# A transformer and state-space block kernel: sums of squares taken in two steps, and unread products in two norm gaps

## What is computed

```python
def rmsnorm(x, g):
    y = x * rsqrt(mean(x * x, axis=-1) + 1e-6)      # mean over the 1024 channels of a token
    return y * g

# first block
...
x = x + rmsnorm(merged @ w_out, norm_mix_post)                 # "post1"
h = rmsnorm(x, norm_mlp_pre)                                   # "n2"
f = square(relu(h @ w_ff_in)) @ w_ff_out
x = x + rmsnorm(f, norm_mlp_post)                              # "post2"
# second block
xn = rmsnorm(x, norm_mix_g_2)                                  # "n3"
...
x = x + merged @ w_out_2
xn2 = rmsnorm(x, norm_ffn_g_2)                                 # "n4"
x = x + (silu(gate) * up) @ w_ffn_out_2
return rmsnorm(x, norm_final_g_2)                              # "n5"
```

## Time and profile before

| | |
|---|---|
| median of three executions | 1516.6 us (1515.08 to 1518.08) |
| the profiled execution, its own time | 1520.02 us |
| its span, first to last instruction | 1518.2 us |
| TensorE (PE) busy | 1435.4 us, 95% |
| VectorE (DVE) busy | 885.6 us, 58% |
| ScalarE (ACT) busy | 626.0 us, 41% |
| mean granted TensorE clock | 0.979 of full |
| chain that ended last | PE 73%, DVE 14%, ACT 9% |

### The profile page before, as it was taken

How to read it: one execution, slowest core, us unless ns; L and a number is a source line. 1 busy time by engine, 2 the same in 40 slices (tenths; PEclk the granted TensorE clock), 3 DMA queues, 4 the chain that set the end, 5 groups by cost and what they waited for, 6 DMA issues and landing times.

```text
span 1518.2 us, 17724 instructions
## 1 busy us (share of the span) xinstructions
PE 1435.4 (95%) x7240; PEld 1155.3 (76%) x7240; DVE 885.6 (58%) x1274; ACT 626.0 (41%) x980; POOL 1.9 (0%) x7
## 2 busy tenths in 40 slices
PE   6999999998999999998999999688899999999997
PEld 5777677777788888887777677576778888888886
DVE  6887644646636354456548786678864443443445
ACT  5452653333313122224326666778743221232232
POOL 0000000000000000000000000000000000000000
PEclk9999999999999999998999999999999999999998
DMA  4222123231333323232121111122232332333232
GB/s 160 84 84 87 55 70 125 85 109 34 111 92 96 105 89 106 86 103 89 58 81 56 56 50 63 38 75 83 71 105 88 97 106 89 97 98 101 94 96 98
DMA packets 36560, 131.62 MB, mean 87 GB/s; under 512 B 4432, under 2 KB 4560, under 8 KB 36224
## 3 DMA queue, kind: packets, MB, share of 16 engines
q1 hardware_dynamic: 36128, 127.16, 26.5%
q0 software_dynamic: 352, 3.34, 0.6%
HBM read 128.39 MB, written 2.10 MB: 86 GB/s over the span
## 4 chain that ended last, share of the span: by engine, by line
PE 73%; DVE 14%; ACT 9%; issue 2%; DMA 1%; SPq 0%; DVEq 0%; ACTq 0%
PE gp L1372 21%; PE gp L1374 21%; PE gp L1373 21%; DVE w_lo L794 2%; PE mp L1548 1%; ACT arena L717 1%; PE mp L1559 1%; PE mp L1517 1%; ACT w_hi L423 1%; DVE arena L1028 1%; PE mp L1398 1%; ACT a_hi L447 1%; ACT arena L572 1%; DVE arena L1035 1%; ACT arena L721 1%
## 5 line engine op out<-in xcount | busy, mean ns | idle before, releaser
L1372 PE MATMUL gp<-a_hi,w_hi 128*128 128x512 f32 x1120 | 444.4, 397 | 14.8 <-DVE arena L1265 13.5
L1373 PE MATMUL gp<-a_lo,w_hi 128*128 128x512 f32 x1120 | 439.7, 393 | 0.0
L1374 PE MATMUL gp<-a_hi,w_lo 128*128 128x512 f32 x1120 | 439.6, 392 | 0.0
L794 DVE TENSOR_TENSOR w_lo<-raw,w_hi 128x1024 fp32r<-128x1024 f32 x232 | 283.4, 1223 | 138.9 <-ACT w_hi L423 137.5
L423 ACT ACTIVATE w_hi<-raw 128x1024 fp32r<-128x1024 f32 x232 | 243.0, 1051 | 204.0 <-PE gp L1374 108.2
L1372 PEld LDWEIGHTS gp<-a_hi,w_hi 128*128 128x128 f32 x1120 | 212.5, 190 | 67.1 <-DVE w_lo L794 17.4
L1374 PEld LDWEIGHTS gp<-a_hi,w_lo 128*128 128x128 f32 x1120 | 212.3, 190 | 44.9
L1373 PEld LDWEIGHTS gp<-a_lo,w_hi 128*128 128x128 f32 x1120 | 212.4, 190 | 43.1
L1372 PE MATMUL gp<-h_hi,w_hi 128*128 128x512 f32 x576 | 225.8, 392 | 8.9 <-DVE h_lo L828 3.4
L1373 PE MATMUL gp<-h_lo,w_hi 128*128 128x512 f32 x576 | 224.9, 391 | 0.0
L1374 PE MATMUL gp<-h_hi,w_lo 128*128 128x512 f32 x576 | 224.8, 390 | 0.0
(11 more groups left out here) (248 smaller groups left out, 1416.6 us busy)
## 6 DMA issues: line engine op xcount, KB each, us to landing
raw<-slabs SPq DMA_DIRECT2D x232, 512.0 KB, 3.5
arena<-x_in SPq DMA_DIRECT2D x4, 512.0 KB, 7.1
arena<-x_in POOLq DMA_DIRECT2D x1, 2048.0 KB, 8.6
out_t<-arena SPq DMA_DIRECT2D x8, 256.0 KB, 2.2
arena<-bias POOLq DMA_DIRECT2D x1, 1024.0 KB, 5.2
arena<-s5b SPq DMA_DIRECT2D x1, 512.0 KB, 8.7
arena<-s5c SPq DMA_DIRECT2D x1, 512.0 KB, 10.1
par<-params SPq DMA_DIRECT2D x1, 232.0 KB, 2.6
```

The lines of the kernel that those rows point to most:

```text
L794: TT(w_lo[:, n % RING, :], raw[:, n % RAW, :], w_hi[:, n % RING, :].bitcast(F32), ALU.subtract).then_inc(w_lo_ready, 1)
L1372: pe.matmul(dst, hi, x_hi(t), start=t == 0, stop=False)
L1373: pe.matmul(dst, hi, x_lo(t), start=False, stop=False)
L1374: ins = pe.matmul(dst, lo, x_hi(t), start=False, stop=t == tiles - 1)
```

## The change

All sums of squares are taken in two functions in place of one: `first_squares` (four calls on `ssum`, after its own wait on `sq_added`) and `last_square` (four calls on chunk 7). For post1, post2 and n5 the first is issued inside the last slab ahead of the gap: after tile 5 of 8 in "out" and "ff", after tile 4 of 6 in "ff2". For n2, n3 and n4 both still stand together. In the gaps of post1 and post2, `keep_clock` issues 1 + 2 + 12 products of 128 by 512 into PSUM bank 4, which nothing reads. On VectorE, `add_square("post2", m - 1)` moves from behind the evacuation of output m to ahead of it.

```diff
 # VectorE, last part of "ff"
                     split(SLAB["ff"] + AHEAD + s0 + FF1_PART + m)
                     if last and m == DC - 1:
                         split(SLAB["q2"] + AHEAD)
+                    if last and m:
+                        add_square("post2", m - 1)
                     src = take("ff", s0 + FF1_PART + m)
                     if p == 0:
                         dve.tensor_copy(Fo[:, m, :], src).then_inc(out_read, 1)
                     else:
                         TT(Fo[:, m, :], Fo[:, m, :], src, ALU.add).then_inc(out_read, 1)
-                    if last and m:
-                        add_square("post2", m - 1)
-                if last:
-                    add_square("post2", DC - 1)
...
 # TensorE
+            def first_squares(kind):
+                pe.wait_ge(sq_added, ADDS * (BY_VEC[kind] + 1))
+                for b in range(T // P):
+                    pe.matmul(mp[:, 5, b:b + 1], ssum[:, b * P:(b + 1) * P], ones[:, 0:1], start=b == 0, stop=False,
+                              skip_group_check=True)
+
+            def last_square(kind):
+                pe.wait_ge(sq_done, 8 * NORM[kind] - PAIRED + DC)
+                for b in range(T // P):
+                    ins = pe.matmul(mp[:, 5, b:b + 1], sq[(DC - 1) % 2][:, b * P:(b + 1) * P], ones[:, 0:1], start=False,
+                                    stop=True, skip_group_check=True)
+                ins.then_inc(rms_sum, 1)
+
             def mean_square(kind):
...
+                first_squares(kind)
+                last_square(kind)
+
+            def keep_clock(name, count):
+                pe.wait_ge(w_lo_ready, SLAB[name] + 1)
+                for _ in range(count):
+                    pe.matmul(mp[:, 4, :], w_hi[:, SLAB[name] % RING, 0:P], h(0), start=True, stop=True)
...
             for k in range(DC):
-                a_stage("out", k, a_wait("merged") if k == 0 else None)
-            mean_square("post1")
+                a_stage("out", k, a_wait("merged") if k == 0 else None,
+                        then={5: lambda: first_squares("post1")} if k == DC - 1 else {})
+            keep_clock("ff", 1)
+            last_square("post1")
+            keep_clock("ff", 2)
             spread("post1")
+            keep_clock("ff", 12)
...
                 for m in range(DC):
                     gemm("ff", s0 + FF1_PART + m, FF1_PART, 1, h, hl,
-                         (lambda t: pe.wait_ge(h_lo_ready, h0 + t + 1)) if m == 0 else None)
+                         (lambda t: pe.wait_ge(h_lo_ready, h0 + t + 1)) if m == 0 else None,
+                         then={5: lambda: first_squares("post2")} if last and m == DC - 1 else {})
...
-            mean_square("post2")
+            keep_clock("q2", 1)
+            last_square("post2")
+            keep_clock("q2", 2)
             spread("post2")
+            keep_clock("q2", 12)
...
                     gemm("ff2", s0 + 2 * chunks + m, chunks, 1, h, hl,
-                         (lambda t: pe.wait_ge(h_lo_ready, H_AT["ff2"] + 8 * part + t + 1)) if m == 0 else None)
+                         (lambda t: pe.wait_ge(h_lo_ready, H_AT["ff2"] + 8 * part + t + 1)) if m == 0 else None,
+                         then={chunks - 2: lambda: first_squares("n5")}
+                         if part == len(FF2_CHUNKS) - 1 and m == DC - 1 else {})
...
-            mean_square("n5")
+            last_square("n5")
             spread("n5")
```

More of the change, by code:

```diff
@@ L1389, in hl @@
                 return h_lo[:, t, :]
-            def mean_square(kind):
[L1393 to L1400, removed]
+            def first_squares(kind):
[9 more added lines that the diff above has]
+                ins.then_inc(rms_sum, 1)
+            def mean_square(kind):
+                first_squares(kind)
[4 more added lines that the diff above has]
+                    pe.matmul(mp[:, 4, :], w_hi[:, SLAB[name] % RING, 0:P], h(0), start=True, stop=True)
             def spread(kind):
@@ L1591, in _, with ff1_part @@
             for k in range(DC):
-                a_stage("out", k, a_wait("merged") if k == 0 else None)
-            mean_square("post1")
+                a_stage("out", k, a_wait("merged") if k == 0 else None,
[3 more added lines that the diff above has]
+            keep_clock("ff", 2)
             spread("post1")
-            def ff1_part(p):
+            keep_clock("ff", 12)
+            def ff1_part(p, last=False):
                 s0, h0 = PART1 * p, H_AT["ff"] + FF1_PART * p
@@ L1603, in ff1_part @@
                     gemm("ff", s0 + FF1_PART + m, FF1_PART, 1, h, hl,
-                         (lambda t: pe.wait_ge(h_lo_ready, h0 + t + 1)) if m == 0 else None)
+                         (lambda t: pe.wait_ge(h_lo_ready, h0 + t + 1)) if m == 0 else None,
+                         then={5: lambda: first_squares("post2")} if last and m == DC - 1 else {})
             start_stage("ff", "n2", START, TOGETHER)
             for p in range(FF1_PARTS):
-                ff1_part(p)
-            mean_square("post2")
+                ff1_part(p, last=p == FF1_PARTS - 1)
+            keep_clock("q2", 1)
+            last_square("post2")
+            keep_clock("q2", 2)
             spread("post2")
+            keep_clock("q2", 12)
             start_stage("q2", "n3", START, TOGETHER)
```

## The result

The changed kernel takes 1522.04 us (median of 13 executions, 1519.52 to 1523.08) where the kernel before, run beside it, takes 1519.1 (13 executions, 1514.86 to 1521.21). The ratio is 1.0027, interval 1.0017 to 1.0037: **about 4 us slower** (2.6 to 5.6 by the interval; the two medians lie 2.9 us apart, the means 3.9). I had forecast no measurable change, 0.05 us faster. With 13 executions in place of three the median of the kernel before is itself 2.5 us above the 1516.6 from which the forecast starts. All ratios here compare ordinary executions; one execution of a later kernel, the changed one with six chunks together, took 8162 us and is in none of them. The profiled execution took 1521.02 us, its span is 1519.2.

The account below looks back on a forecast made before the run. TensorE, busy 95% of the span, was taken as the bound, with VectorE's chain pacing the start stages. Post1 -0.6, post2 +1.3 and n5 -0.75 gave -0.05 us from 1516.6, rounded 1516.5; range 1514.3 to 1519.5.

Parts of the forecast that it names:

- what counts is when VectorE's chain starts: Start stages after post1 and post2: VectorE's low parts set the pace, so the 2.6 us low-clock cost is already hidden.
- rival B: Start stages: TensorE, kept warm, ends them earlier, 2.6 us back in both gaps, total 1511.3 us; chance 0.07.
- So TensorE catches up: Start stage: 12 products take 2.7 us at full clock, VectorE delivers every 2.74 us; TensorE then waits 1.77 us for the last chunk.
- Part 1: First four sums inside the last slab: each slab 0.90 us later, the remaining eight sums 1.0 us with the drain.
- At full clock the step is worth nothing: Splitting the sums: slab cost about equals gap saving, so it pays only where part of the sum ran at half clock.
- Part 2: VectorE's moved addition in "ff": TensorE waits about 1.5 us after tile 5; with 0.9 of sums, the slab ends 2.4 us late.
- Part 3: Unread products in gaps post1 and post2: faster transposes, bounds 0 and -0.52 us; -0.52 taken for post1.
- Their gain is one thing: Unread products' only gain: if the clock is still high, the transposes take 0.60 us instead of 1.12.
- n5: Last sums after "ff2": slab +0.90, about six sums fast and two slow, -1.65; together -0.75 us, bounds -1.0 and -0.1.
- Rival A: Last slab before post2: the stall drops the clock, six products and eight sums run slowly; total +2.05, 1518.6 us; chance 0.24.
- Rival C: Last slab before post2: TensorE doesn't stall for the sixth addition; total -1.55, 1515.0 us; chance 0.11.
- The sign I set for being wrong: Whole kernel: a total beyond 3 us either way would mean a chain other than VectorE's decides in the gaps.

Follow-up runs that it names:

- six chunks together: Start stages take six chunks, not five, for all four outputs at once: ratio 0.9969 on the kernel before, 0.9983 on the changed kernel, both against the kernel before.
- the version with both savings and the products: Kernel before with first four sums moved into the gap's wait, TOGETHER 6 instead of 5, and the 30 unread products: ratio 0.9956 against the kernel before.

## Why the prediction was wrong, point by point

- **Bound now, and what counts is when VectorE's chain starts.** Right as far as it went: the start stage's low clock was hidden, rival B (5 us faster) didn't come about, and chunk 7 came 0.48 us earlier in post1 (forecast 0.6) and 1.40 us later in post2 (forecast 1.3). "So TensorE catches up" was read from the wrong place: 2.7 against 2.74 us gives it 0.04 us a chunk. The room lies further on, where only three products stand between the waits for chunks 6 and 7. The half clock used up the first of these waits (none in post1 before, 1.68 us in the changed kernel), and my "hidden" was right for that reason. What I left out is that a hidden gain isn't free: the idle time it makes lies where the clock can fall.
- **Part 1, first sums in the slab.** Right: +0.90 us in all three, no wait in "out" and "ff2", and eight sums take 1.05. "At full clock the step is worth nothing" holds, and the first sums in the gap show what was given away by putting them into the slab. The 25 ns a product of the Trainium skill ("TensorE: Matmul & The Clock Gate", section Back-to-back issue gap) are not seen here, where each product has a weight load ahead of it: eight took 0.90 us.
- **Part 2, the reordering.** Right in place, cause and size: 1.6 us against 1.5, confirmed by moving the addition. It was called on the path to the end, and it is.
- **Part 3, the unread products: this is the step that failed.** I wrote "Their gain is one thing", priced them between 0 and -0.52 us, and took nothing as their loss at full clock; the sum has no term at all for what happens behind chunk 7. There the changed kernel lost 1.61 and 1.62 us, and the products alone, on the kernel before, 2.53 and 2.67 us (ratio 1.0022). How much of the changed kernel's loss is theirs is less sure: without them it measured 1.0021 against 1.0027, and its trace still has one fall of +1.61 us. The sentence "TensorE still waiting for the last low part at the end of both start stages, longer than 1.77 us" foresaw the longer idle time and drew nothing from it. It had the place slightly wrong too: the wait for chunk 7 was 1.78 us, as before, and the added idle time was a wait for chunk 6, behind which the clock fell. The -0.52 I put to their account was there without them in one trace and partly so in another (0.65 and 1.05 us of transposes against 1.12).
- **n5.** The mechanism was right and the size off: -0.22 in this trace instead of -0.75, since the clock fell less than 0.1 us after the last sums began and not 0.7 (its mean in 1506 to 1508 is 0.93, which puts the fall at 1507.7; the sums began at 1507.66). It lies inside the bounds I gave, -1.0 to -0.1, and the traces fill them: -0.19 to -1.01. Which value a trace has is luck of the fall.
- **Rival A.** A real mechanism, seen in one of four traces with the stall, and not what made the change slower: in the changed kernel's own trace TensorE went through tiles 6 and 7 at full clock. Rival C, no stall, is out.
- **The range.** It held 1514.3 to 1519.5 around a median of 1516.6, so up to +2.9. Every case in it kept the start stages' second half at full clock. Two of its numbers don't follow from the working: the bounds of n5 and of the transposes give -0.3 to +1.1, not -1.0 to +1.5, and the upper end of A was 1519.8.
- **The sign I set for being wrong.** A total beyond 3 us was to mean that a chain other than VectorE's decides in the gaps. The total was beyond 3 us, and in the gaps VectorE's and ScalarE's chain decided as forecast. The loss came after them, when the last chunk was in and TensorE alone had work.

Still open: why the half clock lasted 6.8 us with products alone and 3.4 us in the changed kernel (hence 2.5 to 2.7 us lost against 1.6), and how often each kernel's executions have the fall, since there is one trace a kernel. That two waits are behind the fall is shown by filling them and by taking six chunks together; why in one trace a wait of 0.59 us for chunk 6 went with a fall and in another 0.48 us with none isn't. The kernel without products shows it in one stage of two and measures 1.0021, about as slow as the products alone; more of its executions may have it in both. No run told that apart.

## What to carry to other kernels

Before keeping an engine's clock up through a gap, look at what paces the stage behind it. If that is another engine, the speed only turns into waiting further on; here the 30 products cost 3.3 us on their own, and moving real work into the waits (six chunks together) won 4.7 us with one constant. Work that shares a wait is free, the same work in the full stream of the bounding engine is not: put the early half of a sum into the wait for its late half.

## What the runs showed of the hardware

The clock can fall in the middle of a stage with no idle time over 1.8 us in it. It did so in nine stages of nine in which TensorE waited 0.59 to 1.78 us, ran three products and waited 1.6 to 1.8 us; in four of the nine it fell before the first product behind the second wait, once already 0.6 us after the first wait. One wait of 1.7 to 1.8 us, with none or at most 0.48 us ahead of it, was followed by no fall in eleven stages. Inside the slab of post2, 1.3 us of idle time with 0.9 us of sums behind it went with a fall in one trace of four.

Unread products didn't hold the clock for certain: it fell in the gap all the same in post2 of the changed kernel (0.50 in 710 to 712) and in post1 of the version with both savings and the products (twelve products in 4.24 us). Eight single-column sums take 1.05 us at full clock and 1.84 at half; the same transposes 0.65 and 1.12. Falls elsewhere in the program come and go from one execution to the next, about 1.6 us each. That they are most of why executions of the kernel before lie between 1514 and 1521 us is likely and not shown: the fastest beside the last runs, 1514.0 us, has a mean granted clock of 0.982, the slowest, 1521.17 us, has 0.978.
